# Gathering V rows 12 places behind U rows, with more places for the diagonal weights and earlier query products, in a one-core hybrid attention and PEER layer

## The chip, the cores and the metric

The kernel runs on one core of a Trainium2 chip. The metric is the device time of one execution in microseconds (us), and the number compared is the median over runs. Engines are named as in the profile: PE is TensorE (PEld its weight loads), DVE is VectorE, ACT is ScalarE, POOL is GpSimd, SP is SyncE.

## The reference

One decoder layer over 256 tokens of width 1024, in float32. Attention in two head groups, an output projection, then a product-key expert layer (PEER), which takes most of the time. For each of two chunks of 128 tokens:

```python
q = (xc @ w_query).reshape(PEER_CHUNK, PEER_HEADS, 2, PEER_D_HALF)
sc = jnp.einsum('chpd,hpnd->chpn', q, sub_keys)
s1, i1 = lax.top_k(sc[:, :, 0], 16)
s2, i2 = lax.top_k(sc[:, :, 1], 16)
...
best, pos = lax.top_k(cand, 16)           # of the 256 sums s1 + s2
experts = jnp.take_along_axis(cand_idx, pos, axis=-1)
g = jax.nn.softmax(best, axis=-1)
h = jax.nn.gelu(jnp.einsum('cd,chkd->chk', xc, u[experts]))
return jnp.einsum('chk,chkd->cd', h * g, v[experts])
```

Every token picks 16 experts for each of 8 heads, and each expert is one row of 1024 numbers in `u` and one in `v`. That is 256 gathered tiles of each (2 chunks, 8 heads, 16 choices), a tile being 128 tokens by 1024 numbers, 512 KB.

## The kernel before, in words

No scheduler orders the work: each engine's instructions are written out by hand and the engines meet at semaphores.

**Projection and attention** take the first 160 us or so. Near their end the work on experts begins, so that both overlap on every engine.

**A unit** is one head of one chunk: 16 units, each of 16 rows (gathered tiles), 256 rows in all. Rows are handled in groups of four. For row n the steps are these, each on its own engine and in the order of n:

1. POOL issues the gather of U row n (`gather_u`) into a ring of 10 places (`U_RING`). It waits until the dot product of row n-10 has been taken (`u_used`).
2. DVE takes the dot product of the row with the tokens (`dots`, L1190), after the row has landed, and counts `u_used` up.
3. ACT takes the GELU of a group of four (`gelu(g)`, L814), and DVE multiplies by the gates (`weights(g)`, L1203). DVE's order is `dots` of group g, `weights` of group g-1, then a part of `route`, which finds the experts of a later unit. So no dot product of group g+1 is taken before the GELU of group g-1.
4. ACT writes a 128x128 diagonal with the weight of row n (`diagonal(n)`, L821). ACT's order is `gelu(g)`, then the four diagonals of group g-1. There are 8 places for diagonals (`DIAG_RING`), so diagonal n waits until PE has finished row n-8 (`v_used`).
5. POOL issues the gather of V row n (`gather_v`). Its place is free when PE has finished the row that had it before: 11 rows earlier up to row 103, 13 rows earlier to row 159, and 16 from row 160 (`LATE`) on.
6. PE multiplies the diagonal with the V row into the output sums (`row_product`, L1569), two matmuls of 512 columns that the profile counts as two each, and counts `v_used` up. Five rows near the end (`ADDED_ROWS`) are added by DVE instead.

**POOL's order** is four gathers of U, then four of V, and so on. `LAG` says how far V is behind: the group of V after U rows g..g+3 is that of rows g-8..g-5.

**Queries.** A unit's experts need two query products (`query(e)`, L1487, 8 matmuls counted as 16), each evacuated by ACT (`query_evac`, L773), then a product with the keys (`key_scores`, L1470) and its evacuation (`scores_evac`, L767). Events e = 0 to 15 are the first chunk's, 2 for each head; 16 to 31 the second's. They stand between the row products. In the first chunk, heads 3 to 7 have theirs after rows 10 to 15 of units 0 to 4 on PE, and ACT evacuates two diagonals later. Head 2's (e = 4, 5) stand after rows 4 to 9. Those of the second chunk stand after rows 80 to 143, one event every four rows: query after row 4k, evacuation after diagonal 4k+1, key product after row 4k+2, its evacuation after diagonal 4k+3.

So PE waits for ACT's diagonals, ACT waits for PE's finished rows and queries, DVE waits for ACT's GELU, and POOL waits for both PE (V places) and DVE (U places).

## Time and profile before

| | |
|---|---|
| median of 3 runs | 907.79 us |
| lowest and highest | 902.74 and 909.92 us |
| the profiled execution's own time | 900.53 us |
| its span, first to last instruction | 898.7 us |
| PE, DVE, ACT, POOL busy, share of the span | 78%, 57%, 27%, 56% |
| bytes moved, mean rate | 297.88 MB, 331 GB/s |
| mean granted TensorE clock | 0.891 of 2.4 GHz |

The profile shows one execution. A busy share is over the whole span, and attention and gathers have different limits, so the stages are read one by one. POOL is counted as busy while it makes the descriptors of a gather. Idle time is put before the instruction that follows it, with what ended it; "remote" is the profile's word where it finds no instruction close enough to the release.

### The profile page before, as it was taken

The numbers are of one execution on the slowest core, as the hardware profiler recorded it, in microseconds if no ns is written. First come the engines' busy times: TensorE is split into PE (matmuls) and PEld (weight loads), VectorE is DVE, ScalarE is ACT, GpSimd is POOL, SyncE is SP. The second block draws the span as 40 slices with busy tenths as digits, with TensorE's granted clock in tenths as the row PEclk, the third lists the DMA queues.
The fourth block names the chain that finished last, engine by engine and source line by source line (L and its number), as shares of the span: only waits on it lengthen the run. The fifth ranks groups of instructions, "written<-read, shape, count | busy, mean of one in ns | idle before, by whom it ended". The sixth has DMA issues, their size and how long they took to land.

```text
span 898.7 us, 7608 instructions
## 1 busy us (share of the span) xinstructions
PE 699.5 (78%) x2208; PEld 376.9 (42%) x2208; DVE 510.1 (57%) x1395; ACT 243.0 (27%) x599; POOL 500.2 (56%) x533
## 2 busy tenths in 40 slices
PE   7989956879978877866686687788577857847877
PEld 5778645444434443433343343443233323312332
DVE  5754468638837474734554563557556764746643
ACT  6676434133131313012012121133030212121210
POOL 4000055646666666665654665556757666756763
PEclk9999988979999897968889998999769778968988
DMA  8856177989999999998987998979989999999996
GB/s 331 269 178 233 49 280 275 355 275 343 406 407 409 409 397 358 370 359 296 371 307 255 371 347 320 358 263 373 411 293 411 350 361 370 380 352 385 369 349 262
DMA packets 90087, 297.88 MB, mean 331 GB/s; under 512 B 8761, under 2 KB 14018, under 8 KB 90050
## 3 DMA queue, kind: packets, MB, share of 16 engines
q0 software_dynamic: 73728, 268.47, 79.6%
q1 hardware_dynamic: 16306, 28.97, 9.2%
q8 instruction: 16, 0.26, 0.1%
q14 instruction: 21, 0.17, 0.1%
q10 hardware_dynamic: 16, 0.00, 0.0%
HBM read 296.36 MB, written 1.05 MB: 331 GB/s over the span
## 4 chain that ended last, share of the span: by engine, by line
PE 60%; issue 15%; another core or an unknown queue 14%; ACT 6%; DVE 3%; DMA 1%; SPq 0%; DVEq 0%; ACTq 0%
PE bank L1569 44%; PE bank L1487 5%; PE bank L1301 4%; PE xg L1434 2%; PE bank L1434 2%; ACT diag L821 1%; DMA w_raw<-in_w_in_dram 1%; PE bank L1470 1%; DVE u_row L1190 1%; PE bank L1322 1%; PE bank L1350 1%; ACT soft L656 1%; ACT w_hi L601 1%; ACT L814 1%
## 5 line engine op out<-in xcount | busy, mean ns | idle before, releaser
L1569 PE MATMUL bank<-v_row,diag 128*128 128x512 f32 x1002 | 495.0, 643 | 148.7 <-issue 94.9
L1569 PEld LDWEIGHTS bank<-v_row,diag 128*128 128x128 f32 x1002 | 197.9, 206 | 398.1 <-issue 327.7
L541 POOL DMA_INDIRECT v_row<-in_peer_v_dram,expert x256 | 241.7, 944 | 179.1 <-remote 66.4
L527 POOL DMA_INDIRECT u_row<-in_peer_u_dram,expert x254 | 241.5, 951 | 109.2 <-issue 70.2
L1190 DVE CUSTOM_DVE_ANT_0 u_row<-u_row,xg 128x1024 f32<-128x1024 f32 x254 | 295.3, 1214 | 11.8 <-DMA u_row<-in_peer_u_dram,expert 8.3
L821 ACT ACTIVATE diag<-ident,act_w 128x128 f32<-128x128 f32 x251 | 87.6, 392 | 206.5 <-remote 87.2
L1203 DVE TENSOR_TENSOR act_w<-h_gelu,gate 128x4 f32<-128x4 f32 x64 | 10.5, 164 | 205.9 <-ACT h_gelu L814 121.5
L773 ACT ACTIVATE qT<-bank 128x128 f32<-128x128 f32 x32 | 8.8, 276 | 225.6 <-remote 178.7
L1487 PE MATMUL bank<-featT,wq_rest 128*128 128x128 f32 x192 | 29.6, 291 | 19.4 <-issue 19.2
L1487 PEld LDWEIGHTS bank<-featT,wq_rest 128*128 128x128 f32 x192 | 27.1, 204 | 27.7 <-issue 27.7
L428 POOL TENSOR_TENSOR normed<-qk_raw,t_qk_rs 128x512 f32<-128x512 f32 x4 | 4.1, 1048 | 56.5 <-DVE t_qk_rs L1026 56.5
L767 ACT ACTIVATE scores<-bank,t_rstd 128x128 f32<-128x128 f32 x32 | 11.8, 368 | 86.2 <-PE bank L1470 63.8
L1128 DVE MAX8 key_val<-scores 128x8 f32<-128x128 f32 x62 | 15.2, 283 | 34.4 <-issue 14.5
L1301 PE MATMUL bank<-w_hi,xn_hi 128*128 128x512 f32 x80 | 32.8, 410 | 2.4 <-ACT qk_raw L636 2.4
L1301 PE MATMUL bank<-w_hi,xn_lo 128*128 128x512 f32 x80 | 32.0, 400 | 0.0
L1301 PE MATMUL bank<-w_lo,xn_hi 128*128 128x512 f32 x80 | 31.8, 398 | 0.0
L902 DVE TENSOR_TENSOR w_lo<-w_raw,w_hi 128x2048 fp32r<-128x2048 f32 x11 | 25.2, 2287 | 8.4 <-ACT w_hi L601 8.4
L1470 PEld LDWEIGHTS bank<-skT,qT 128*128 128x128 f32 x64 | 14.1, 226 | 27.4 <-issue 20.7
L1487 PEld LDWEIGHTS bank<-featT,wq 128*128 128x128 f32 x192 | 23.4, 194 | 4.5 <-issue 4.4
L527 POOL DMA_INDIRECT u_first<-in_peer_u_dram,expert x2 | 2.1, 1050 | 41.1 <-DVE expert L1091 39.7
L814 ACT ACTIVATE h_gelu<-h_dot 128x4 f32<-128x4 f32 x64 | 12.5, 197 | 43.6 <-DVE h_dot L1190 36.5
L1487 PE MATMUL bank<-featT,wq 128*128 128x128 f32 x192 | 23.6, 277 | 0.0
(198 smaller groups left out, 624.7 us busy)
## 6 DMA issues: line engine op xcount, KB each, us to landing
w_raw<-in_w_in_dram SPq DMA_DIRECT2D x11, 1024.0 KB, 9.4
w_raw<-in_w_out_dram SPq DMA_DIRECT2D x4, 1024.0 KB, 5.1
v_row<-in_peer_v_dram,expert POOLq DMA_INDIRECT x256
u_row<-in_peer_u_dram,expert POOLq DMA_INDIRECT x254
wq<-in_peer_w_query_dram SPq DMA_DIRECT2D x3, 1024.0 KB, 9.2
wq_rest<-in_peer_w_query_dram SPq DMA_DIRECT2D x1, 3072.0 KB
x_sb<-in_x_dram SPq DMA_DIRECT2D x2, 512.0 KB, 4.8
w_raw<-in_w_in_dram SPq DMA_DIRECT2D x2, 512.0 KB, 6.4
```

Source lines behind the costliest of these rows:

```text
L527: pool.indirect_dma_start(u_row(n)[:, :], None, peer_u[0], bass.IndirectOffsetOnAxis(ap=expert[:, u, s:s + 1], axis=0))\
L541: pool.indirect_dma_start(v_row(n)[:, :], None, peer_v[0], bass.IndirectOffsetOnAxis(ap=expert[:, u, s:s + 1], axis=0))\
L814: act.activation(h_gelu[:, u % 4, s:s + GROUP], h_dot[:, u % 4, s:s + GROUP], ACT.Gelu).then_inc(gelu_done, 1)
L821: act.activation(diag[:, m % DIAG_RING, :], ident[:, :], ACT.Copy, scale=act_w[:, u % 4, s:s + 1])\
L902: dve.tensor_tensor(w_lo[:, j % W_PARTS, :, :].rearrange("p k n -> p (k n)"), w_raw[:, j % W_LOADS, :], w_hi[:, j % W_PARTS, :, :].rearran ...
L1128: at[a] = mark(dve.max(key_val[:, r2, a, top], score[a]))
L1190: dve.tensor_tensor_reduce(out=row[:, :], in0=row[:, :], in1=xg_row, scale=1.0, scalar=0.0, op0=ALU.mult, op1=ALU.add, accum_out=h_dot[:, ...
L1301: ins = mm(ps[bank][:, :], a[:, 4 * kh + k, h * P:(h + 1) * P], b[:, j % W_PARTS, k, :], start=kh == 0 and k == 0 and n == 0, stop=kh == 1 ...
L1434: ins = mm(ps[x2_bank(h, c)][:, :], mixT[h][:, 4 * kh + k, :], w_raw[:, j % W_LOADS, k * COLS:(k + 1) * COLS], start=h == 0 and kh == 1 an ...
L1470: mm(ps[2 + e % 2][:, 0:P], qT[:, e % 2, :], skT[:, hp, :], start=True, stop=True).then_inc(scores_done, 1)
L1487: ins = mm(ps[2 + e % 2][:, 0:P], wq_block(i, k, c), featT[h][:, k, :], start=k == 0, stop=k == KD - 1)
L1569: ins = mm(ps[y_bank(h, c)][:, :], diag[:, m % DIAG_RING, :], v_row(n)[:, c * COLS:(c + 1) * COLS], start=False, stop=True, skip_group_che ...
```

## The change

The lag of V behind U grows from 8 rows to 12. The diagonals get 12 places for rows before 160: the 8 of before (`diag_sq`) and 4 in the space of `mixed`, a tile of attention that is read for the last time by its last transposes. From row 160 there are 16: the first 8, and 8 more (`diag_freed`) in the space of a V place that the late rows don't use. At the crossing, diagonals 160 to 163 take places last used by rows 156 to 159. The queries and key products of head 2 stand ahead of all V rows on PE, and their evacuations ahead of the first GELU on ACT, with a wait for the last transposes of `mixed`. The queries of heads 3 to 7, and the transposes of the second chunk's features, stand four rows earlier. The queries of the second chunk stay where they were.

```diff
-DIAG_RING = 8
+DIAG_FIRST = 8
+DIAG_EARLY = 12
 GROUP = 4
-LAG = 8
+LAG = 12
...
-    diag = Region(sq_at).put("diag", [P, DIAG_RING, P])
+    diag_sq = Region(sq_at, sq_at + 4 * K).put("diag_sq", [P, DIAG_FIRST, P])
+    diag_mixed = Region(mixed_at, mixed_at + 2 * K).put("diag_mixed", [P, DIAG_EARLY - DIAG_FIRST, P])
...
+    freed = LATE - len(ring) + TOPK - 12
+    diag_freed = Region(v_row_at[v_place[freed]]).put("diag_freed", [P, TOPK - DIAG_FIRST, P])
+    diag_all = [diag_sq[:, i, :] for i in range(DIAG_FIRST)]
+    diag_all += [diag_mixed[:, i, :] for i in range(DIAG_EARLY - DIAG_FIRST)]
+    diag_all += [diag_freed[:, i, :] for i in range(TOPK - DIAG_FIRST)]
+    diag_turn = [m % DIAG_EARLY for m in range(LATE)]
+    diag_turn += [m % TOPK if m % TOPK < DIAG_FIRST else m % TOPK + DIAG_EARLY - DIAG_FIRST for m in range(LATE, GATHERS)]
+
+    def diag_before(m):
+
+        first = freed if diag_turn[m] >= DIAG_EARLY else -1
+        return max((i for i in range(m) if diag_turn[i] == diag_turn[m]), default=first)
...
-                need(act, v_used, m - DIAG_RING + 1)
+                need(act, v_used, diag_before(m) + 1)
...
+            act.wait_ge(probsT_done, MIXES_LAST + 1)
             d_deviation(1)
+            query_evac(4)
+            query_evac(5)
+            scores_evac(4)
+            scores_evac(5)
             for g in range(GROUPS + 1):
...
-                        if n == 56:
+                        if n == 52:
                             feat_evac(1, 0)
...
                         if 0 <= u <= 4:
                             e = 2 * (u + 3)
-                            if at == 10:
+                            if at == 6:
                                 query_evac(e)
-                            if at == 12:
+                            if at == 8:
                                 query_evac(e + 1)
-                            if at == 13:
+                            if at == 9:
                                 scores_evac(e)
-                            if at == 15:
+                            if at == 11:
                                 scores_evac(e + 1)
...
+            head_queries(2)
...
-                if n == 52:
+                if n == 48:
                     pe.wait_ge(scores_ready, 12)
...
                 if u <= 4:
                     e = 2 * (u + 3)
-                    if at == 10:
+                    if at == 6:
                         query(e)
```

The same shift of four rows is made for the other three places of the last hunk, and what stood for e = 4 and 5 after rows 4 to 9 is taken out on both engines.

POOL, the first gathers of V. `u_row` and `v_row` are the places of the two rings. Before:

```order
L527 DMA u_row0_136<-in_peer_u_dram,expert_93 128x1024
L527 DMA u_row1_137<-in_peer_u_dram,expert_93 128x1024
L541 DMA v_row0_148<-in_peer_v_dram,expert_93 128x1024
L541 DMA v_row1_149<-in_peer_v_dram,expert_93 128x1024
L541 DMA v_row11_159<-in_peer_v_dram,expert_93 128x1024
L541 DMA v_row12_160<-in_peer_v_dram,expert_93 128x1024
L527 DMA u_row2_138<-in_peer_u_dram,expert_93 128x1024
```

POOL, the same place of the changed kernel:

```order
L543 DMA u_row0_137<-in_peer_u_dram,expert_93 128x1024
L543 DMA u_row1_138<-in_peer_u_dram,expert_93 128x1024
L543 DMA u_row2_139<-in_peer_u_dram,expert_93 128x1024
L543 DMA u_row3_140<-in_peer_u_dram,expert_93 128x1024
L543 DMA u_row4_141<-in_peer_u_dram,expert_93 128x1024
L543 DMA u_row5_142<-in_peer_u_dram,expert_93 128x1024
L557 DMA v_row0_149<-in_peer_v_dram,expert_93 128x1024
```

The gathers of U rows 12 to 15 now stand ahead of V row 0, and every later group of V stands four U rows further back.

PE, from the identity products that end the attention to the first V rows. Before:

```order
L1547 MATMUL bank1<-scaled_108,ident_49 128x512
L1569 MATMUL bank0<-v_row0_148,diag_126 128x512
L1569 MATMUL bank1<-v_row0_148,diag_126 128x512
L1569 MATMUL bank0<-v_row1_149,diag_126 128x512
L1569 MATMUL bank1<-v_row1_149,diag_126 128x512
```

PE, the same place of the changed kernel:

```order
L1559 MATMUL bank1<-scaled_108,ident_49 128x512
L1499 MATMUL bank2<-featT0_122,wq2_low_132 128x128 x4
L1499 MATMUL bank2<-featT0_122,wq2_high_133 128x128 x4
L1499 MATMUL bank3<-featT0_122,wq2_low_132 128x128 x4
L1499 MATMUL bank3<-featT0_122,wq2_high_133 128x128 x4
L1482 MATMUL bank2<-skT_107,qT_81 128x128
L1482 MATMUL bank3<-skT_107,qT_81 128x128
L1582 MATMUL bank0<-v_row0_149,diag_sq_126 128x512
```

Head 2's two queries (`wq2`) and its two key products (`skT`) moved from between rows 4 and 9 to ahead of row 0.

ACT, from the first GELU on; `qT` is an evacuated query, `gexp` the exponential of the gates. Before:

```order
L814 ACTIVATE h_gelu_98<-h_dot_97 128x4 x2
L821 ACTIVATE diag_126<-ident_49,act_w_99 128x128 x4
L814 ACTIVATE h_gelu_98<-h_dot_97 128x4
L821 ACTIVATE diag_126<-ident_49,act_w_99 128x128 x3
L773 ACTIVATE qT_81<-bank2 128x128
L821 ACTIVATE diag_126<-ident_49,act_w_99 128x128
```

ACT, the same place of the changed kernel:

```order
L691 ACTIVATE t_d_sd_73<-t_d_ms_72 128x4
L789 ACTIVATE qT_81<-bank2 128x128
L789 ACTIVATE qT_81<-bank3 128x128
L783 ACTIVATE scores0_124<-bank2,t_rstd2_78 128x128
L783 ACTIVATE scores0_124<-bank3,t_rstd2_78 128x128
L830 ACT_TABLE_LOAD
L830 ACTIVATE h_gelu_98<-h_dot_97 128x4 x2
L837 ACTIVATE diag_sq_126<-ident_49,act_w_99 128x128 x4
L830 ACTIVATE h_gelu_98<-h_dot_97 128x4
L837 ACTIVATE diag_sq_126<-ident_49,act_w_99 128x128 x4
```

Four evacuations now stand ahead of the first GELU, and the first eight diagonals have no evacuation between them.

## Rows read from the trace of the kernel before

**Rows 1.** Page, costliest groups: busy, mean ns | idle before, what ended it.

```profile
L1569 PE MATMUL bank<-v_row,diag 128*128 128x512 f32 x1002 | 495.0, 643 | 148.7 <-issue 94.9
...
L541 POOL DMA_INDIRECT v_row<-in_peer_v_dram,expert x256 | 241.7, 944 | 179.1 <-remote 66.4
...
L1190 DVE CUSTOM_DVE_ANT_0 u_row<-u_row,xg 128x1024 f32<-128x1024 f32 x254 | 295.3, 1214 | 11.8 <-DMA u_row<-in_peer_u_dram,expert 8.3
```

**Rows 2.** Windows: length, PE PEld DVE ACT POOL busy, clock, DMA share, GB/s.

```profile
112.00:210.00 98.00, 71.81 (x313) 47.11 (x312) 64.45 (x217) 30.30 (x81) 53.92 (x58) 0.84 0.83 298
210.00:325.00 115.00, 101.98 (x287) 49.99 (x286) 70.86 (x207) 30.23 (x79) 76.21 (x81) 0.96 1.02 400
325.00:400.00 75.00, 54.36 (x162) 28.86 (x161) 41.37 (x117) 12.87 (x39) 50.23 (x54) 0.82 0.97 365
400.00:620.00 220.00, 166.70 (x559) 88.20 (x558) 115.33 (x329) 48.26 (x140) 126.44 (x136) 0.91 0.89 327
620.00:890.00 270.00, 196.92 (x401) 81.48 (x400) 157.87 (x406) 51.21 (x137) 178.50 (x187) 0.85 0.96 367
```

**Rows 3.** Groups on POOL, from 112 to 210 us.

```profile
L527 POOL DMA_INDIRECT u_row<-in_peer_u_dram,expert x32 | 30.1, 941 | 17.5 <-issue 7.9 <-DVE h_dot L1190 6.5 <-DVE expert L1167 2.4
L541 POOL DMA_INDIRECT v_row<-in_peer_v_dram,expert x24 | 22.6, 940 | 24.7 <-PE bank L1313 8.6 <-remote 6.0 <-issue 5.5
```

**Rows 4.** Groups on POOL, from 325 to 400 us.

```profile
L527 POOL DMA_INDIRECT u_row<-in_peer_u_dram,expert x27 | 25.8, 956 | 8.2 <-issue 7.3 <-DVE h_dot L1190 0.9
L541 POOL DMA_INDIRECT v_row<-in_peer_v_dram,expert x27 | 25.4, 940 | 16.9 <-issue 7.0 <-remote 6.6 <-PE bank L1569 3.3
```

**Rows 5.** Groups on POOL, from 400 to 620 us.

```profile
L527 POOL DMA_INDIRECT u_row<-in_peer_u_dram,expert x68 | 63.9, 940 | 37.9 <-issue 19.9 <-DVE h_dot L1190 18.0
L541 POOL DMA_INDIRECT v_row<-in_peer_v_dram,expert x68 | 63.9, 940 | 56.0 <-PE bank L1569 22.3 <-remote 19.0 <-issue 14.6
```

**Rows 6.** Groups on POOL, from 620 to 890 us.

```profile
L541 POOL DMA_INDIRECT v_row<-in_peer_v_dram,expert x99 | 94.1, 950 | 55.6 <-issue 29.1 <-remote 24.8 <-PE bank L1569 1.5
L527 POOL DMA_INDIRECT u_row<-in_peer_u_dram,expert x88 | 84.6, 961 | 33.7 <-issue 25.6 <-DVE h_dot L1190 8.1
```

**Rows 7.** Waits, 620 to 890 us: who waited for whom, total, times, longest.

```profile
POOL v_row L541 <- remote: 24.8, 10, 4.1
```

**Rows 8.** Timeline, 157 to 189 us: start, length, engine, what, idle before.

```profile
157.32 0.30 ACT L814 ACTIVATE h_gelu<-h_dot 128x4 f32<-128x4 f32 x2
157.52 3.32 PE L1547 MATMUL bank<-scaled,ident 128*128 128x512 f32 x4
...
159.21 0.94 POOL L527 DMA_INDIRECT u_row<-in_peer_u_dram,expert  x1 [1.90 <-DVE h_dot L1190]
...
170.16 1.06 PE L1487 MATMUL bank<-featT,wq_high 128*128 128x128 f32 x8
...
184.54 0.28 ACT L773 ACTIVATE qT<-bank 128x128 f32<-128x128 f32 x1 [19.44 <-remote]
...
188.19 0.16 DVE L1203 TENSOR_TENSOR act_w<-h_gelu,gate 128x4 f32<-128x4 f32 x1 [14.90 <-ACT h_gelu L814]
```

**Rows 9.** Timeline around query 21, 469 to 478 us: PE, ACT, POOL.

```profile
469.75 1.06 PE L1487 MATMUL bank<-featT,wq_high 128*128 128x128 f32 x8
...
477.52 0.28 ACT L773 ACTIVATE qT<-bank 128x128 f32<-128x128 f32 x1 [10.85 <-remote]
...
477.81 0.94 POOL L541 DMA_INDIRECT v_row<-in_peer_v_dram,expert  x1 [2.71 <-remote]
```

**Rows 10.** Timeline, 791 to 802 us: ACT and POOL.

```profile
791.76 0.40 ACT L821 ACTIVATE diag<-ident,act_w 128x128 f32<-128x128 f32 x1 [10.09 <-issue]
...
796.98 0.94 POOL L527 DMA_INDIRECT u_row<-in_peer_u_dram,expert  x1 [0.30 <-issue]
...
801.62 0.40 ACT L821 ACTIVATE diag<-ident,act_w 128x128 f32<-128x128 f32 x1 [9.37 <-remote]
...
801.80 0.94 POOL L541 DMA_INDIRECT v_row<-in_peer_v_dram,expert  x1 [3.88 <-remote]
```

More of the change, by code:

```diff
@@ L75 @@
 MIX_AFTER = {0: 0, 4: 1, 6: 4}
+MIXES_LAST = max(MIXES_READY)
 D_VALUES = [1, 5]
@@ L819, in diagonal @@
                 m = multiplied(n)
-                need(act, v_used, m - DIAG_RING + 1)
-                act.activation(diag[:, m % DIAG_RING, :], ident[:, :], ACT.Copy, scale=act_w[:, u % 4, s:s + 1])\
+                need(act, v_used, diag_before(m) + 1)
+                act.activation(diag_all[diag_turn[m]], ident[:, :], ACT.Copy, scale=act_w[:, u % 4, s:s + 1])\
                    .then_inc(diag_ready, 1)
@@ L876, in _ @@
                                 scores_evac(e)
-                        if n == GATHERS // 2 + DIAG_RING:
+                        if n == GATHERS // 2 + DIAG_FIRST:
                             for c in range(2):
@@ L1568, in row_product @@
                 for c in range(2 if n < GATHERS - 1 else 1):
-                    ins = mm(ps[y_bank(h, c)][:, :], diag[:, m % DIAG_RING, :],
+                    ins = mm(ps[y_bank(h, c)][:, :], diag_all[diag_turn[m]],
                              v_row(n)[:, c * COLS:(c + 1) * COLS],
@@ L1593, in _ @@
                     x2_transposes(1, 1)
-                if n == 57:
+                if n == 53:
                     pe.wait_ge(featT_ready[0], 3)
-                if n == 4:
-                    query(4)
-                if n == 6:
-                    query(5)
-                if n == 7:
-                    key_scores(4)
-                if n == 9:
-                    key_scores(5)
                 if u <= 4:
                     e = 2 * (u + 3)
-                    if at == 10:
+                    if at == 6:
                         query(e)
-                    if at == 12:
+                    if at == 8:
                         query(e + 1)
-                    if at == 13:
+                    if at == 9:
                         key_scores(e)
-                    if at == 15:
+                    if at == 11:
                         key_scores(e + 1)
```

9 lines of the change are left out of this document (removed).

## The prediction

> **What bounds the kernel now.** I first read the costliest groups [rows 1] to find the long stage: 256 gathers of V, as many of U, 254 listed dot products, and 1002 listed matmuls (about 250 rows of four) that PE is busy with for 495 us, 1.98 us a row. None of that fills the span of 898.7 us. Next come the windows [rows 2], which tell where the transfers are full. From 210 to 325 us they run at 400 GB/s with a DMA share of 1.02: there the gathers themselves are the bound. Elsewhere it is 298, 365, 327 and 367 GB/s, so something keeps POOL from issuing.
>
> What that is worth can be counted. One gather takes POOL 0.94 us plus 0.30 us of idle time before it even where nothing is waited for [rows 1, 10], 1.24 us together. Idle time beyond 0.30 us a gather is true waiting. From 112 to 210 us (56 gathers) it is 42.2 - 16.8 = 25.4 us [rows 3]; from 325 to 400 us (54) 25.1 - 16.2 = 8.9 us [rows 4]; from 400 to 620 us (136) 93.9 - 40.8 = 53.1 us [rows 5]; from 620 to 890 us (187) 89.3 - 56.1 = 33.2 us [rows 6]. In the last stage nearly all of it stands before V gathers, and ten waits on "remote" hold 24.8 us, the longest 4.1 us [rows 7].
>
> What is POOL waiting for there? ACT makes one diagonal at 791.76 us and the next only at 801.62, after 9.37 us of waiting; then POOL, idle since 797.92, gets its V place at 801.80 [rows 10]. Diagonal and place both wait for rows that PE has finished. A query's matmuls end at 470.81 us, ACT takes the result at 477.52, and POOL's V place comes at 477.81 after 2.71 us of idling [rows 9]. So what PE has done is told to the others up to 7 us late while POOL issues without a break, and comes through some 3 us after POOL has stopped. The Trainium skill (TensorE: Matmul & The Clock Gate, "The cost: per-tile semaphore tail") gives tens of nanoseconds for a matmul's semaphore increment. By that, ACT would have gone on at about 470.9; this trace shows 6.7 us more, and the row decides. I take the lateness as given, whatever makes it: the places are then a stock on which POOL lives until the news arrives.
>
> **The change part by part, against the profiled execution's 900.5 us.** The median of the runs is 907.79, or 1.008 times that.
>
> *Queries of head 2 ahead of all V rows.* Removed: ACT's wait for query 4, 19.44 us until 184.54, in whose shadow DVE waited 14.90 us for a GELU [rows 8]. Added: ACT's first GELU, at 157.32 before, now comes behind four evacuations, and these behind PE's identity products, which end at 160.84 [rows 8]. Two queries follow: half of one is 1.06 us [rows 8], so 4.2 us by the rows; consecutive halves overlap a little, and I take 3.7. Then key product, evacuations and a table load, which I estimate at 2.5 us, so the GELU runs at about 167, 10 us late. Behind it stand the weights of group 0 and the dot product of row 8, on which the gather of U row 18 depends; that row was issued at 159.21 [rows 8] and now comes at about 168.8. In the new order POOL has by 157 us issued what needs no GELU, U rows 0 to 17 and V rows 0 to 3, 22 gathers, and idles 12 us. From 168.8 it can go on without a wait, since the experts of unit 2 are found early and ACT has no evacuation among the first eight diagonals: to 208.7 us that is 39.9 / 1.245 + 1 = 33, or 55 in all. Before, 57 were issued by then, among them the 56 of [rows 3]. Two gathers less are 2.5 us. Bounds: if the wait for query 4 simply returns elsewhere, the 12 us stay lost; if the twelve places spare a later wait of this stage, 5 us are won. I take +2.
>
> *210 to 325 us.* The transfers are full [rows 2], so neither lag nor places matter: 0. A gather only comes earlier or later in the stream.
>
> *325 to 400 us, and the start of the next stage.* A V place waits for PE's row 11 back, and in the new order POOL has issued four more U gathers when it gets to that V gather. A stretch between two long waits holds about 16 gathers (54 issued in 3 to 4 stretches), then 20. If each wait is still some 3 us long, 4/20 of 8.9 us go, 1.8. The same holds for the first 40 us of the next stage, until row 104 has 13 places: a fifth of 53.1 us, of which another fifth goes, 2.1. Together -4; between 0 and -13.
>
> *400 to 620 us, queries of the second chunk.* These stay where they are, and ACT is never more than two rows ahead of PE there. When ACT waits for the query after row 4k, the GELU of group k+1 is done, so DVE can take dot products up to row 4k+15 and POOL can issue U up to row 4k+25. With the lag of 8, POOL stops at V row 4k+13, having issued U to 4k+23: 8k+37 gathers. With 12 it stops at U row 4k+26, having issued V to 4k+11: 8k+38. The wait changes its name from V to U and nothing is won: 0; between +5 (POOL four V gathers behind where DVE sets the pace) and -10.
>
> *620 to 890 us, 16 diagonals.* Here no evacuation ties ACT to PE. With 8 places ACT stops 8 rows ahead of the last row it has been told of; PE then runs dry too, and the news that ends the wait brings few rows. With 16, PE works on, so that each release frees more places, and the lag adds four U gathers to each stretch. Ten remote waits [rows 7], several of them in pairs, are about eight stretches of 187 / 8 = 23 gathers. I take 12 more a stretch, between 4 (the lag alone) and 20: 33.2 x 12/35 = 11.4 us. Bounds: 4/27 of it, 5 us, and all of it, 33 us. At the crossing, diagonals 160 to 163 wait for rows 156 to 159: one wait of the usual 3 us, within these bounds.
>
> *The end.* Twelve V gathers instead of eight follow the last U gather, but the number of all gathers is the same, and the last V row waits for no dot product: 0. *Other edits:* the wait for the last transposes of `mixed` is met before it is reached, since ACT has evacuated later ones. Moving queries of heads 3 to 7 up by four rows keeps the scores as early as before against the U rows, though V is later: 0, and without it DVE would wait for scores by four rows, 10 us a unit.
>
> Sum: +2 - 4 + 0 - 11.4 = -13.4, so 887.1 us for the execution and 894.3 for the median, taken as 894.
>
> **The rivals.** *The wait only changes its name everywhere.* U has 10 places still, and DVE's dot products wait for GELUs that stand behind diagonals. If these set the pace in the last stage too, what remains is the start, +2, and some saving of the middle: 900 or so, 908 as a median. For it speaks that in the stage at 400 to 620 us U gathers wait 18.0 us for dot products [rows 5]; against it that from 620 on it is 8.1 us [rows 6].
>
> *Slower: the start is not regained.* POOL's 12 idle us stand just ahead of the stage in which transfers are full. If the news of PE's rows is late again among rows 6 to 11, where head 3's queries now stand, the stretch from 168.8 to 208.7 us has two waits of 3 to 4 us that I left out, and the stage at 400 us gives the +5. Then 900.5 + 2.5 + 7 + 5 - 2 = 913, or 920 as a median. It decides from one such wait on, if the last stage gives only its 5 us.
>
> *The waits of the last stage go altogether,* if the news is late by a fixed time and the longer stock outlasts it: 900.5 + 2 - 4 - 33 = 865.5, as a median 872. Against it: the waits are all near 3 us, up to 4.1 at most [rows 7], though the stretches differ, which looks like an end that POOL's own pause brings.
>
> *No room in the transfers.* If memory gave about 350 GB/s at most, all stages from 325 us on would be full and only the start would count, 903, or 910 as a median. The Trainium skill (DMA: Bandwidth & Descriptors, "Where 436 GB/s comes from") says that about 358 GB/s per core binds such loads. The windows show 400 over 115 us [rows 2], so I give this little.
>
> **How the numbers follow.** Runs of this kernel differ by 0.8% between lowest and highest, so 1% is about what a measurement can tell. Forecast (all with 1 to 2.5% gained) 0.41; waits gone altogether 0.12; only the name changes 0.25; no room 0.03; slower 0.19. Faster by over 1% is 0.41 + 0.12 = 0.53; within 1%, 0.25 + 0.03 = 0.28; slower 0.19. The range takes in most of the case of 872 and ends between the unchanged time and 920: 873 to 914.
>
> **What would show each step.** Right: POOL idle from about 157 to 168 us, then no wait over 1 us until 200; ACT without a wait of over 10 us before 200; from 400 to 620 us the idle time before V gathers falls and that before U gathers rises by as much, the sum within 10 us; from 620 on, waiting beyond 0.30 us a gather is near 22 us, with stretches over 30 gathers, and ACT's diagonals wait far less. Wrong: POOL's waits before 210 us add up to over 30 us; or the last stage still has ten remote waits; or the rate there stays at 367 GB/s with POOL never waiting.

## The result: slower, 948.83 us against 907.79

The changed kernel takes 948.83 us (median of 5 runs, 936.89 to 949.47). Against the kernel before on the same chip that is 1.044, 95% interval 1.038 to 1.050. The forecast was 894 us, in a range of 873 to 914. The profiled execution is that of the median and has a span of 947.0 us, 48.3 us more than before, and a mean granted clock of 0.873 after 0.891. (The medians are only 41.0 us apart, since the profiled execution of the kernel before was 7 us faster than its median.)

The costliest groups of the changed kernel, which answer to [rows 1] (L543 gathers U, L557 gathers V, L1202 takes the dot products, L830 the GELU, L1215 makes the weights, L789 evacuates a query):

```profile
L543 POOL DMA_INDIRECT u_row<-in_peer_u_dram,expert x254 | 240.4, 946 | 218.2 <-DVE h_dot L1202 145.2
...
L557 POOL DMA_INDIRECT v_row<-in_peer_v_dram,expert x256 | 242.4, 947 | 117.7 <-issue 70.7
...
L1215 DVE TENSOR_TENSOR act_w<-h_gelu,gate 128x4 f32<-128x4 f32 x64 | 10.5, 164 | 227.3 <-ACT h_gelu L830 206.4
...
L789 ACT ACTIVATE qT<-bank 128x128 f32<-128x128 f32 x32 | 8.9, 277 | 295.7 <-remote 234.9
```

Before, the longer idle time stood ahead of the V gathers (179.1 us, [rows 1]). Now it stands ahead of the U gathers, and two thirds of it end with a dot product of DVE. DVE waited 206.4 us for GELUs, and ACT, which makes them, 234.9 us for "remote" at its query evacuations. As the timeline further down shows, those are the links of one chain. The windows answer to [rows 2]:

```profile
112.00:210.00 98.00, 66.27 (x290) 43.82 (x289) 59.27 (x201) 29.00 (x75) 48.17 (x51) 0.79 0.76 279
210.00:325.00 115.00, 98.10 (x273) 47.31 (x273) 70.47 (x207) 25.67 (x72) 72.52 (x78) 0.94 0.97 373
325.00:400.00 75.00, 55.61 (x165) 27.99 (x163) 38.96 (x106) 14.71 (x39) 47.68 (x51) 0.91 0.94 353
400.00:640.00 240.00, 170.39 (x556) 91.10 (x556) 113.05 (x314) 44.25 (x131) 122.74 (x131) 0.86 0.77 288
640.00:935.00 295.00, 211.96 (x419) 87.06 (x419) 166.63 (x434) 57.16 (x156) 192.63 (x202) 0.82 0.95 363
```

Windows of two kernels don't hold the same work. So I counted POOL's 512 gathers in their order in both traces and read when the n-th was issued; the difference of two columns says where the time went:

| n-th gather | before | after | later by | added in this stretch |
|---|---|---|---|---|
| 60 | 212.4 | 220.7 | 8.3 | 8.3 |
| 100 | 269.3 | 277.7 | 8.4 | 0.1 |
| 200 | 417.3 | 437.6 | 20.3 | 11.9 |
| 300 | 574.4 | 611.1 | 36.7 | 16.4 |
| 340 | 637.8 | 684.1 | 46.3 | 9.6 |
| 400 | 724.4 | 769.7 | 45.3 | -1.0 |
| 512 | 886.6 | 931.9 | 45.3 | 0.0 |

8 us are lost by the 60th gather and 38 from the 100th to the 340th, in which the queries lie. The last stage begins at about the 340th gather. I hoped to win 11 us in it, and from there to the last gather it takes 248.8 us before and 247.8 after. From the last gather to the end of the span it is 12.1 us before and 15.1 after. The waits of the changed kernel from 400 to 640 us show the chain (who waited for whom, total, times, longest):

```profile
DVE act_w L1215 <- ACT h_gelu L830: 131.4, 12, 18.6
ACT qT L789 <- remote: 94.6, 7, 18.8
POOL u_row L543 <- DVE h_dot L1202: 84.3, 22, 16.1
...
POOL v_row L557 <- PE bank L1582: 1.5, 5, 0.3
```

Here are POOL's groups from 112 to 210 us, then from 400 to 640, then from 640 to 935; they answer to [rows 3], [rows 5] and [rows 6]:

```profile
L543 POOL DMA_INDIRECT u_row<-in_peer_u_dram,expert x30 | 28.2, 941 | 31.8 <-DVE h_dot L1202 24.4 <-issue 6.8 <-PE bank L1313 0.6
L557 POOL DMA_INDIRECT v_row<-in_peer_v_dram,expert x20 | 19.0, 951 | 10.6 <-issue 5.8 <-remote 4.8
...
L543 POOL DMA_INDIRECT u_row<-in_peer_u_dram,expert x66 | 62.1, 940 | 97.8 <-DVE h_dot L1202 84.3 <-issue 13.4
L557 POOL DMA_INDIRECT v_row<-in_peer_v_dram,expert x65 | 61.3, 942 | 19.8 <-issue 18.3 <-PE bank L1582 1.5
...
L557 POOL DMA_INDIRECT v_row<-in_peer_v_dram,expert x108 | 102.7, 951 | 55.4 <-issue 29.6 <-remote 21.5 <-PE bank L1582 4.4
L543 POOL DMA_INDIRECT u_row<-in_peer_u_dram,expert x94 | 89.9, 957 | 44.8 <-issue 24.7 <-DVE h_dot L1202 17.6 <-remote 2.6
```

In the query stage the waits for PE's rows, 22.3 + 19.0 us before [rows 5], are down to 1.5; those for dot products are up from 18.0 to 84.3. The wait did change its name, as forecast, but it became longer in doing so: beyond 0.30 us a gather it is 117.6 - 131 x 0.30 = 78.3 us for 131 gathers, after 53.1 for 136.

One stop shows why. This is the timeline around query 21 (engine, what, idle time before):

```profile
486.97 0.97 PEld L1499 LDWEIGHTS bank<-featT,wq_high 128*128 128x128 f32 x8
487.08 1.06 PE L1499 MATMUL bank<-featT,wq_high 128*128 128x128 f32 x8
...
496.22 0.94 POOL L543 DMA_INDIRECT u_row<-in_peer_u_dram,expert  x1 [0.30 <-issue]
500.16 0.28 ACT L789 ACTIVATE qT<-bank 128x128 f32<-128x128 f32 x1 [16.17 <-remote]
...
505.03 0.37 ACT L783 ACTIVATE scores<-bank,t_rstd 128x128 f32<-128x128 f32 x1 [4.01 <-PE bank L1482]
505.41 1.28 ACT L824 ACT_TABLE_LOAD   x1
...
506.94 1.28 ACT L830 ACT_TABLE_LOAD   x1
508.23 0.21 ACT L830 ACTIVATE h_gelu<-h_dot 128x4 f32<-128x4 f32 x1
...
508.47 0.16 DVE L1215 TENSOR_TENSOR act_w<-h_gelu,gate 128x4 f32<-128x4 f32 x1 [18.20 <-ACT h_gelu L830]
...
511.81 1.21 DVE L1202 CUSTOM_DVE_ANT_0 u_row<-u_row,xg 128x1024 f32<-128x1024 f32 x1
...
513.30 0.94 POOL L543 DMA_INDIRECT u_row<-in_peer_u_dram,expert  x1 [16.14 <-DVE h_dot L1202]
```

PE's query ends at 488.14. POOL goes on issuing until 497.16, and 3.0 us after it has stopped ACT gets the news, 12.0 us after the query's end. With that news the stop is not over: POOL stands at a U gather, and a U place comes free last of all, after the evacuation, the key product, the scores (505.03), two table loads of 1.28 us, the GELU (508.23), the weights and DVE's next top-k work (until 511.81) and the dot product. That is 13.1 us behind the news. Before, around the same query, POOL stood at a V gather and went on 0.29 us after ACT had the news, 477.81 after 477.52 [rows 9]. This is not the one case: nine query evacuations of the kernel before are followed by a V gather that ends a wait 0.29 or 0.30 us later, while in the changed kernel four late ones (at 427.31, 500.16, 585.66 and 617.70 us) are followed by a U gather 9.0 to 13.1 us later. By the order of the program the next V gathers stand behind the U gather in POOL's one queue, though the next two, rows 112 and 113, need no row of PE after row 100, which was done ahead of the query.

### The profile page after: what moved, and what is told of

Same layout as the page of the kernel before. It is cut to its first block, busy times and chain, and to the rows that moved or that the text cites. A ratio compares the mean times of both kernels' runs of the same rounds, so it can differ in the third digit from the quotient of the medians.

```text
span 947.0 us, 7608 instructions
## 1 busy us (share of the span) xinstructions
PE 713.8 (75%) x2208; PEld 380.5 (40%) x2208; DVE 511.8 (54%) x1395; ACT 241.1 (25%) x599; POOL 499.9 (53%) x533
## 3 DMA queue, kind: packets, MB, share of 16 engines
HBM read 296.36 MB, written 1.05 MB: 314 GB/s over the span
## 4 chain that ended last, share of the span: by engine, by line
PE 51%; issue 17%; another core or an unknown queue 15%; DVE 9%; ACT 4%; DMA 2%; POOL 1%; SPq 0%; DVEq 0%; ACTq 0%
PE bank L1582 35%; DVE u_row L1202 5%; PE bank L1313 4%; PE bank L1499 4%; PE xg L1446 1%; PE bank L1382 1%; DMA v_row<-in_peer_v_dram,expert 1%; PE bank L1362 1%; POOL u_row L543 1%; PE bank L1334 1%; PE bank L1482 1%; ACT diag_sq L837 1%; DMA x_sb<-in_x_dram 1%; ACT L830 1%
## 5 line engine op out<-in xcount | busy, mean ns | idle before, releaser
L1582 PE MATMUL bank<-v_row,diag_sq 128*128 128x512 f32 x624 | 314.1, 651 | 110.6 <-ACT diag_sq L837 58.8
L543 POOL DMA_INDIRECT u_row<-in_peer_u_dram,expert x254 | 240.4, 946 | 218.2 <-DVE h_dot L1202 145.2
L1202 DVE CUSTOM_DVE_ANT_0 u_row<-u_row,xg 128x1024 f32<-128x1024 f32 x254 | 296.7, 1215 | 37.7 <-DMA u_row<-in_peer_u_dram,expert 34.6
L557 POOL DMA_INDIRECT v_row<-in_peer_v_dram,expert x256 | 242.4, 947 | 117.7 <-issue 70.7
L1582 PEld LDWEIGHTS bank<-v_row,diag_sq 128*128 128x128 f32 x624 | 125.2, 208 | 266.1 <-issue 196.4
L1582 PE MATMUL bank<-v_row,diag_freed 128*128 128x512 f32 x170 | 97.0, 698 | 48.9 <-issue 48.9
L1215 DVE TENSOR_TENSOR act_w<-h_gelu,gate 128x4 f32<-128x4 f32 x64 | 10.5, 164 | 227.3 <-ACT h_gelu L830 206.4
L1582 PE MATMUL bank<-v_row,diag_mixed 128*128 128x512 f32 x208 | 104.9, 639 | 29.6 <-issue 18.8
L789 ACT ACTIVATE qT<-bank 128x128 f32<-128x128 f32 x32 | 8.9, 277 | 295.7 <-remote 234.9
L837 ACT ACTIVATE diag_sq<-ident,act_w 128x128 f32<-128x128 f32 x156 | 53.5, 391 | 119.5 <-remote 78.9
L1582 PEld LDWEIGHTS bank<-v_row,diag_freed 128*128 128x128 f32 x170 | 36.8, 217 | 106.8 <-issue 106.1
L1582 PEld LDWEIGHTS bank<-v_row,diag_mixed 128*128 128x128 f32 x208 | 40.2, 204 | 76.2 <-issue 63.6
L830 ACT ACTIVATE h_gelu<-h_dot 128x4 f32<-128x4 f32 x64 | 12.7, 200 | 96.8 <-issue 58.7
L1499 PEld LDWEIGHTS bank<-featT,wq_rest 128*128 128x128 f32 x192 | 24.4, 197 | 11.0 <-issue 11.0
L1499 PE MATMUL bank<-featT,wq_rest 128*128 128x128 f32 x192 | 24.6, 279 | 3.7 <-issue 3.6
```

Of the source, the lines that this page charges most:

```text
L543: pool.indirect_dma_start(u_row(n)[:, :], None, peer_u[0], bass.IndirectOffsetOnAxis(ap=expert[:, u, s:s + 1], axis=0))\
L557: pool.indirect_dma_start(v_row(n)[:, :], None, peer_v[0], bass.IndirectOffsetOnAxis(ap=expert[:, u, s:s + 1], axis=0))\
L830: act.activation(h_gelu[:, u % 4, s:s + GROUP], h_dot[:, u % 4, s:s + GROUP], ACT.Gelu).then_inc(gelu_done, 1)
L837: act.activation(diag_all[diag_turn[m]], ident[:, :], ACT.Copy, scale=act_w[:, u % 4, s:s + 1])\
L1202: dve.tensor_tensor_reduce(out=row[:, :], in0=row[:, :], in1=xg_row, scale=1.0, scalar=0.0, op0=ALU.mult, op1=ALU.add, accum_out=h_dot[:, ...
L1215: dve.tensor_tensor(act_w[:, u % 4, s:s + GROUP], h_gelu[:, u % 4, s:s + GROUP], gate[:, u % 2, s:s + GROUP], ALU.mult).then_inc(act_ready, 1)
```

## Experiments

Theory A is what the timeline suggests: with V 12 rows behind, POOL meets a U gather at the stops of the query stage, and U waits for the longest chain. The rivals: the start (head 2's queries ahead) carries the cost (B), or the places of the diagonals do (C).

**The parts alone, on a chip where the kernel before takes 801.75 us.** c1 is the changed kernel with `LAG = 8`. c2, c3 and c4 are the kernel before with one part of the change each: the distance, head 2's queries ahead (what stood for them after rows 4 to 9 is taken out), and the places of the diagonals.

```diff
-LAG = 12
+LAG = 8
```

> The changed kernel with the lag of V put back from 12 to 8, all else as changed. Theory A (with the longer lag POOL stops at a U gather, which is set free last in the chain of late rows, diagonals, GELU, dot product, while V places that are free stand behind it): the loss of 41 us goes, 900 to 915 us, and U gathers wait under 25 us for dot products between 400 us and V row 160. Theory B (the loss is made at the start, by head 2's queries ahead of the first GELU, and by the queries moved up): stays at 930 to 950 us. Theory C (with more places ACT and DVE run ahead and get in PE's way): 930 to 950 us.

```diff
-LAG = 8
+LAG = 12
```

> The kernel before with the lag of V alone set to 12; 8 places for diagonals and all queries where they were. Theory A: 940 to 965 us, at least as slow as the changed kernel, since scores also come four rows late against U. Theory B: 900 to 915 us. Theory C: 900 to 915 us.

```diff
             d_deviation(1)
+            query_evac(4)
+            query_evac(5)
+            scores_evac(4)
+            scores_evac(5)
...
             head_queries(1)
...
+            head_queries(2)
```

> The kernel before with head 2's queries, key products and evacuations alone moved ahead of all V rows and of the first GELU. Theory A: 903 to 915 us, the first GELU some 10 us later, most of it regained by 210 us. Theory B: 930 us or more. Theory C: as before, within 5 us.

```diff
-                need(act, v_used, m - DIAG_RING + 1)
-                act.activation(diag[:, m % DIAG_RING, :], ident[:, :], ACT.Copy, scale=act_w[:, u % 4, s:s + 1])\
+                need(act, v_used, diag_before(m) + 1)
+                act.activation(diag_all[diag_turn[m]], ident[:, :], ACT.Copy, scale=act_w[:, u % 4, s:s + 1])\
```

> The kernel before with the places for diagonals alone changed, 12 to row 159 and 16 from there. Theory A: 893 to 908 us, less waiting of ACT from 620 us on and a little won there. Theory B: as before, within 5 us. Theory C: 930 us or more.

Measured against the kernel before: c1 1.005 (1.003 to 1.007), c2 1.007 (1.005 to 1.010), c3 1.005 (1.003 to 1.008), c4 1.000 (0.999 to 1.001). The expectations were set for 908 us and missed in all their times. None of the theories is told from the others here: on this chip there is little to lose.

**Both kernels on another chip of that kind** (the kernel before 801.48 us), unchanged:

> The changed kernel itself, run beside the kernel before on the chip of this call. If the 4.4% belong to the change wherever it runs: ratio 1.04. If they come from PE's finished work being told late, which the four runs so far don't show (a query is evacuated 0.04 us after its last matmul in each of 30 cases of the run with lag 8, and the kernel before takes 801.75 us there): about the sum of the lag alone and the start alone, ratio 1.01, 808 to 813 us, as long as this chip tells PE's work at once; and 1.04 if it tells it late.

> The kernel before, unchanged, for its trace on this chip. If PE's work is told at once: 800 to 803 us, transfers at about 409 GB/s from 210 us to the end, and no query evacuated more than 1 us after its last matmul. If it is told late: 900 to 912 us and a trace like the first one.

The changed kernel takes 1.011 (1.009 to 1.013) of the time before, the kernel before again 1.000. The timeline of the kernel before on this chip, at a query:

```profile
409.99 1.06 PE L1487 MATMUL bank<-featT,wq_high 128*128 128x128 f32 x8
...
411.08 0.28 ACT L773 ACTIVATE qT<-bank 128x128 f32<-128x128 f32 x1 [5.53 <-PE bank L1487]
```

and its window from 400 to 620 us:

```profile
400.00:620.00 220.00, 179.33 (x546) 88.10 (x545) 147.89 (x401) 55.30 (x156) 160.95 (x171) 0.97 1.03 409
```

ACT takes the query 0.04 us after its matmuls end, in the middle of POOL's issuing, and so it is at every query from the fifth on. Transfers run at 409 GB/s (327 in [rows 2]) and bound the kernel. So the lateness that I took as given is seen on some chips and not on others, and where it is seen the kernel takes some 100 us more. That the lateness makes all of these is not shown: the granted clock differs as well, 0.940 here and 0.891 in the first trace. Even here the mechanism is seen once, started by another delay; the changed kernel's timeline:

```profile
368.67 2.56 PE L1582 MATMUL bank<-v_row,diag_mixed 128*128 128x512 f32 x4 [4.11 <-DMA v_row<-in_peer_v_dram,expert]
...
374.10 0.28 ACT L789 ACTIVATE qT<-bank 128x128 f32<-128x128 f32 x1 [15.85 <-PE bank L1499]
...
378.25 0.16 DVE L1215 TENSOR_TENSOR act_w<-h_gelu,gate 128x4 f32<-128x4 f32 x1 [9.75 <-ACT h_gelu L830]
...
381.91 0.94 POOL L543 DMA_INDIRECT u_row<-in_peer_u_dram,expert  x1 [6.99 <-DVE h_dot L1202]
```

PE waited 4.11 us for a V row to land, the query behind it came later by that, and POOL stopped at a U gather for 6.99 us.

**Making the news late on purpose.** If the lateness is what the cost hangs on, it should appear where it is put in. A detour: SP waits for PE's signal and sends a DMA of 64 B; POOL's V gathers and ACT's diagonals (where they wait for rows from 80 on) and the 16 query evacuations of the second chunk wait for its landing instead. e1 is the kernel before with this detour, e2 the changed kernel, e3 the changed kernel with `LAG = 8`.

```diff
-                need(pool, v_used, v_before(n) + 1)
+                need_row(pool, v_before(n) + 1)
...
-                act.wait_ge(query_done, e + 1)
+                if e >= HP:
+                    act.wait_ge(told_query[e % 4], 16 * ((e - HP) // 4 + 1))
+                else:
+                    act.wait_ge(query_done, e + 1)
...
+                sp.wait_ge(seen, value)
...
+                sp.dma_start(relay[at:at + 1, 16 * slot:16 * slot + 16], x[0, 0:1, 0:16]).then_inc(told_on, 16)
```

> The kernel before, in which from the 80th row on the news of PE's finished work goes by a detour: SP waits for v_used (and for query_done of the second chunk) and passes it on by a small DMA of 64 B whose landing POOL's V gathers, ACT's diagonals and ACT's query evacuations wait for. Nothing of the work changes; what PE has finished is known to POOL and ACT some us later. Theory A (the cost is lateness times the length of the chain that a stopped U gather hangs on): V places and diagonals come free late but the V gathers stop in small pieces, as on the first chip; 1.00 to 1.02 of the kernel before. The rival (late news costs both kernels the same): the same 1.00 to 1.02 here, so this run is the base for the next two.

> The changed kernel with the same detour. Theory A: the ratio to the kernel before grows clearly past the 1.011 of the changed kernel without a detour, and more than that of the kernel before with the detour grows past 1: 1.025 to 1.045, with POOL's waits for DVE's dot products at U gathers each after a run of 16 gathers between 380 and 620 us. The rival (late news costs both the same, the 4.4% of the first chip came from something else): 1.011 plus what the detour costs the kernel before, within 0.005.

> The changed kernel with LAG = 8 and the same detour: V eight rows behind U again, the diagonals and the start as changed. Theory A: 8 rows behind undo most of what the detour adds to the changed kernel; the ratio comes within 0.008 of the kernel before with the detour. If the diagonals or head 2's queries carry the cost under late news, it stays near the changed kernel with the detour.

Measured, the kernel before at 800.25 us: e1 1.032 (1.030 to 1.035), e2 1.052 (1.048 to 1.056), e3 1.041 (1.038 to 1.044). With the detour a query of the second chunk is taken 1.2 to 4.7 us after its last matmul. POOL's groups from 400 to 620 us, of e1, then e2, then e3:

```profile
L565 POOL DMA_INDIRECT u_row<-in_peer_u_dram,expert x78 | 73.1, 937 | 26.1 <-issue 16.5 <-DVE h_dot L1231 9.7
L579 POOL DMA_INDIRECT v_row<-in_peer_v_dram,expert x78 | 73.1, 937 | 49.0 <-DMA relay<-in_x_dram 23.8 <-issue 19.8 <-DVE h_dot L1231 5.4
...
L581 POOL DMA_INDIRECT u_row<-in_peer_u_dram,expert x74 | 69.8, 944 | 62.4 <-DVE h_dot L1243 49.0 <-issue 13.4
L595 POOL DMA_INDIRECT v_row<-in_peer_v_dram,expert x74 | 69.3, 937 | 22.6 <-issue 22.6
...
L581 POOL DMA_INDIRECT u_row<-in_peer_u_dram,expert x77 | 72.4, 940 | 25.9 <-issue 18.9 <-DVE h_dot L1243 7.0
L595 POOL DMA_INDIRECT v_row<-in_peer_v_dram,expert x76 | 71.5, 941 | 51.3 <-DMA relay<-in_x_dram 25.1 <-issue 23.7 <-DVE h_dot L1243 2.5
```

This is the picture of the first chip, made smaller on a chip that doesn't have it: at 8 rows behind POOL waits for V places, at 12 only for dot products, and longer (49.0 us against 23.8 + 5.4 + 9.7 and 25.1 + 2.5 + 7.0). The changed kernel's distance to the kernel before grows from 1.1% to 1.9% (1.052 / 1.032); that of e3 is 0.8%, at the edge of the 0.008 expected. So of the 1.9%, 1.1 hang on the distance. The direction is Theory A's, but the sizes were missed: 1.052 lies above its 1.025 to 1.045, and e1 had gone past its 1.02. A detour of 1.2 to 4.7 us does not make 4.4%.

**The queries' news alone, and later news.** f1 (the kernel before) and f2 (the changed kernel) detour the query evacuations alone; SP still sends its DMAs for the rows, so what these cost is in the result. f3 and f4 (again before and changed) have the whole detour, but a row is told with the last of its four only, and a query behind the next row. These four ran on a chip of the first pair's kind: the kernel before took 899.98 us.

```diff
-                need_row(pool, v_before(n) + 1)
+                need(pool, v_used, v_before(n) + 1)
...
-                need_row(act, m - DIAG_RING + 1)
+                need(act, v_used, m - DIAG_RING + 1)
```

> The kernel before with the detour for the 16 query evacuations of the second chunk alone: V gathers and diagonals wait for PE's own signal again; SP's small DMAs for the rows are still sent, but nobody waits for them. If the query's step (query, qT, key scores, scores, then the GELU behind it on ACT) carries what late news costs, this stays near the 1.032 of the full detour (1.02 or more); if late V places carry it, it is within 1.005 of 1.

> The changed kernel with the detour for the second chunk's query evacuations alone. Theory A, in the form that a stopped U gather hangs on the query's step and V has reserve: 1.035 to 1.052, most of what the full detour costs the changed kernel, and more above the kernel before with the same detour than the 1.1% without any. If the rows' news are what the difference hangs on, it comes within 0.005 of 1.011.

```diff
-                i = value - TOLD_FROM - 1
+                i = min((value - TOLD_FROM - 1) | 3, multiplied(GATHERS) - TOLD_FROM - 1)
```

> The kernel before with the detour, and the news made later: a V row's place and diagonal are told with the last row of its four only, a query with the row behind it (one row is about 2.5 us). Theory A: the kernel before loses more than by the plain detour, 1.04 to 1.07, the V gathers stopping first.

> The changed kernel with the same later news. Theory A (cost is lateness times the chain of a stopped U gather): its distance to the kernel before with the same news grows beyond the 1.9% of the plain detour, to 2.5 to 4%. The rival (a fixed difference, the places of the changed kernel being enough to hide the rest): it stays at 1 to 2% or shrinks, since diagonals have 12 and 16 places.

Measured: f1 1.027 (1.018 to 1.036), f2 1.073 (1.065 to 1.081), f3 1.077 (1.065 to 1.089), f4 1.091 (1.082 to 1.101). The detour of the queries alone, with SP's DMAs, costs the kernel before 2.7%. The distance of f2 to f1 is 4.5% (1.073 / 1.027), about the 4.4% of the first pair over again: on a chip with late news it does not grow by the detour, and f2 lies above the 1.035 to 1.052 expected. And f4 stands only 1.3% above f3, where Theory A expected 2.5 to 4. The intervals of the two overlap, and f3's four runs spread from 961.61 to 978.51 us, so the 1.3% is rough; but nothing here bears out the form "cost is lateness times chain". With news in fours POOL stops at V gathers of f3 for 87.0 us of the 220 from 400 on. I take it that the advantage of stopping at V is used up there.

f2 also shows who is told late, since here SP waits for PE as well. The timeline of SP's queue, from 488 to 512 us, then from 504 to 508, then ACT and POOL:

```profile
488.52 18.05 SPq L521 DMA_DIRECT2D relay<-in_x_dram  x5
...
506.01 0.57 SPq L521 DMA_DIRECT2D relay<-in_x_dram  x2
...
502.12 0.94 POOL L573 DMA_INDIRECT u_row<-in_peer_u_dram,expert  x1 [0.30 <-issue]
509.27 0.28 ACT L822 ACTIVATE qT<-bank 128x128 f32<-128x128 f32 x1 [19.48 <-DMA relay<-in_x_dram]
...
521.95 0.94 POOL L573 DMA_INDIRECT u_row<-in_peer_u_dram,expert  x1 [18.89 <-DVE h_dot L1235]
```

PE's query had ended at 493.94; SP passed nothing on between 494 and 506, and its next two messages left from 506.01 on, 2.95 us after POOL's last gather before them ended at 503.06. (The view merges the five messages of its first line into one of 18.05 us.) SP's other wait, for the landing of an earlier message, was over by 492.47. So SP, too, hears of PE's work only when POOL has paused: the lateness is not one of ACT's or POOL's receiving alone.

**The parts alone again, on a chip of the first kind** (the kernel before 897.21 us), with the edits of c2 and c1:

> The kernel before with LAG = 12 alone, as c2, again, for the case that this chip tells PE's work late (the kernel before near 900 us): then Theory A (the distance carries the cost, since a stopped U gather waits for the longest chain) expects 1.03 to 1.05; if the start or the diagonals carry it, 1.01. Where the kernel before is near 800 us: 1.007 as before.

> The changed kernel with LAG = 8, as c1, again, for the same case. Theory A on a chip with late news: 1.00 to 1.015, most of the 4.4% gone. If the start (head 2's queries ahead) or the diagonals carry the 4.4%: 1.03 or more. Where the kernel before is near 800 us: 1.005 as before.

Measured: **g1, the distance alone, 1.077** (1.068 to 1.085), above the 1.03 to 1.05 expected; **g2, everything but the distance, 1.004** (1.000 to 1.009), within its 1.00 to 1.015. POOL's groups from 400 to 620 us, of g1, then of g2:

```profile
L541 POOL DMA_INDIRECT v_row<-in_peer_v_dram,expert x61 | 57.2, 937 | 23.1 <-issue 17.7 <-remote 4.8 <-PE bank L1569 0.6
L527 POOL DMA_INDIRECT u_row<-in_peer_u_dram,expert x60 | 56.2, 937 | 84.9 <-DVE h_dot L1190 71.3 <-issue 13.6
...
L557 POOL DMA_INDIRECT v_row<-in_peer_v_dram,expert x68 | 63.7, 936 | 57.8 <-PE bank L1582 27.4 <-remote 15.5 <-issue 14.9
L543 POOL DMA_INDIRECT u_row<-in_peer_u_dram,expert x67 | 63.0, 940 | 38.2 <-issue 19.2 <-DVE h_dot L1202 19.0
```

One number in the source, 12 for 8, moves the stops from V to U, and 121 gathers go out in 220 us where 135 did. From the 200th to the 340th gather g1 takes 255.3 us and g2 226.3; from there to the last they take 249.9 and 248.9. That decides for the distance, against B and C: the start and the places together cost 0.4% here (0.0 to 0.9), a tenth of the 4.4. With the distance of 12 they give back some of what the distance costs, 7.7% down to 4.4 (measured on two chips), 8.8 us of it by the 100th gather (286.5 in g1, 277.7 in the changed kernel). In that stretch the wait that I had removed, query 4's, stands in g1's timeline with a U gather behind it:

```profile
190.22 0.28 ACT L773 ACTIVATE qT<-bank 128x128 f32<-128x128 f32 x1 [28.17 <-remote]
...
204.65 0.94 POOL L527 DMA_INDIRECT u_row<-in_peer_u_dram,expert  x1 [18.96 <-DVE h_dot L1190]
```

How much of what they give back is the places and how much the earlier queries was not tried.

**The other way.** The kernel before with a distance of 4 (e4, on the chip of e1, and h1), and the changed kernel with 4 (h2). Both chips were of the faster kind (the kernel before at 800.25 and at 800.71 us).

```diff
-LAG = 8
+LAG = 4
```

> The kernel before with LAG = 4: V gathers four rows behind U, the way opposite to the change, nothing else. Theory A, on a chip that tells PE's work at once: a stop costs only where the transfers run dry, and a V row that has landed early waits for its diagonal longer, so V places stop more often; 0.995 to 1.01. If a shorter distance goes on helping, below 0.995; a rival (each row of distance costs 0.2% at the end of the kernel, because four V gathers and their products stand behind the last U row): 0.993, 4 rows of 2 x 1.25 us less after the last U gather.

> The kernel before with LAG = 4, as e4. Theory A: the V gathers stand nearer behind their U gathers, so a stop falls on V even more often; where the news is late (the kernel before near 900 us) it expects 0.985 to 1.005, since the V gathers, with fewer landed rows in reserve, stop sooner but release sooner. The rival (both stops cost the same; the distance of 12 is only past the reach of the places): 0.995 to 1.02, worse than LAG = 8, since V places stay taken while their diagonals are missing. Where the kernel before is near 800 us: 1.002 as before.

> The changed kernel with LAG = 4: the diagonals' places and head 2's queries as changed, the distance 4. Whether more diagonals help a short distance: with 8 rows behind they were worth nothing (1.004 with the start on the late chip), and with 12 rows behind the changed kernel stood at 1.044 against 1.077 of the distance alone. Theory A: within 0.01 of h1, plus or minus the start's 0.005. A version that beats both kernels would show here or in h1 as under 0.99.

Measured: e4 1.002 (1.001 to 1.004), h1 1.003 (1.002 to 1.004), h2 1.004 (1.002 to 1.006). So on the faster kind 8 is the best of the three distances, by a little (12: 1.007), and no version ran faster than the kernel before by more than the noise (c4, 1.000, comes nearest). What 4 does where the news is late stays open.

## Why the prediction was wrong

**The failed step is the term of the query stage**, "the wait changes its name from V to U and nothing is won: 0; between +5 and -10". The count behind it (8k+37 gathers against 8k+38) was right: in the changed kernel each of the seven stops of over 7 us between 400 and 660 us comes when 8k+38 gathers are out (198, 222, 238, 254, 286, 302 and 318), and in the kernel before the long stops at V come within two gathers of 8k+37. But I counted how many gathers go out before a stop and took it that every stop ends alike. Its end is what differs: a V place comes with PE's news, 0.3 us after ACT has it; a U place 9 to 13 us later. From the 200th to the 340th gather 26.0 us are lost, five times my bound. g1 and g2 show that the distance is the cause; that it acts by this chain is read from the timelines and from e2, where the waits move to U as soon as the news is late.

The size of the lateness was misread as well. I wrote "up to 7 us late" from one query; in the same trace the query that ends at 372.48 us is evacuated at 389.12, 16.6 us later. None of my terms had a lateness of that size.

**325 to 400 us, -4:** the same step, taken with the wrong sign. I gave each wait "some 3 us" by the V waits of [rows 4], and saw the stretches grow; from the 100th to the 200th gather (269 to 417 us before) 11.9 us are lost.

**The start, +2:** 8.3. The GELU ran at 160.32 rather than 167, and POOL went on at 162.21 rather than 168.8, better than I had worked out. But the slower rival's condition came true. The changed kernel's timeline:

```profile
201.26 0.28 ACT L789 ACTIVATE qT<-bank 128x128 f32<-128x128 f32 x1 [29.08 <-remote]
...
201.55 0.94 POOL L557 DMA_INDIRECT v_row<-in_peer_v_dram,expert  x1 [4.83 <-remote]
...
212.03 0.94 POOL L543 DMA_INDIRECT u_row<-in_peer_u_dram,expert  x1 [8.29 <-DVE expert L1179]
```

Head 3's query, now among rows 6 and 8, waits for late news as head 2's did (29.08 us after 19.44 in [rows 8]), and the weights, top-k work and experts of unit 2 behind it come at 211.76, where I had them "found early". On a chip without lateness c3 shows 0.5% for this part alone.

**The last stage, -11.4:** -1.0 from the 340th gather on. The stretches did not grow as I took it. With stops of over 1 us counted, those within eight gathers as one, POOL stops eight times in these 172 gathers before and seven times after, so a mean stretch goes from 22 to 25 gathers, where I had 23 and 35. The waits of the changed kernel from 640 to 935 us:

```profile
ACT diag_sq L837 <- remote: 78.9, 11, 27.3
...
POOL v_row L557 <- remote: 21.5, 6, 5.6
...
POOL u_row L543 <- DVE h_dot L1202: 17.6, 12, 7.5
```

The remote waits at V fell from ten to six, but they last up to 5.6 us rather than 4.1 [rows 7]: 21.5 us after 24.8. Waiting beyond 0.30 us a gather is 55.4 + 44.8 - 202 x 0.30 = 39.6 us in this window, where I said 22. But the window holds a stop of 7.5 us at 657 us that still belongs to the queries. From the 340th gather on the same sum is 32.5 us before and 31.7 after. (Of the 33.2 us before, 7.3 stood before U gathers, in one wait of 7.2, so "nearly all of it stands before V gathers" was too much said.) ACT's remote waits for diagonals are fewer and longer (11, the longest 27.3 us, after 19 of up to 10.1), and yet the 16 places and the lag together won POOL no more than the 1.0 us. I had written that the lateness ends with POOL's pause, and still priced each wait at its old length. That a longer stock of places only makes the news later is how I read this; it was not tried by itself. c4 (1.000, the places alone) and g2 (1.004, with the start) show it worth nothing at 8 rows behind, on either kind of chip.

**The end, 0:** +3.0 us behind the last gather. What of it the four more V rows make was not tried.

**The rivals.** "Only the name changes" was right on where the waits of the query stage go and wrong on what they cost. The slower rival had the start right (its condition came true, and its 2.5 + 7 us stand against the measured 8.3), but it again capped the query stage at +5, so 920 fell short by 29 us. That the waits vanish, or that 350 GB/s bound the kernel, is refuted: 373 GB/s from 210 to 325 us here, 409 on the chips of the faster kind. The Trainium skill's figure of about 358 GB/s per core (DMA: Bandwidth & Descriptors, "Where 436 GB/s comes from") lies below both. The Trainium skill's tens of nanoseconds for a semaphore increment (TensorE: Matmul & The Clock Gate, "The cost: per-tile semaphore tail") agree with the 0.04 us of those chips, not with the 12.0 us here.

## What to carry to other kernels

Where one in-order queue issues for several rings, ask at each stop which ring it stands at, and follow the chain from the event that ends the stop to that ring's release; counting how far the queue gets before it stops is half of the sum. Here a larger distance moved the stop to the ring that is released last, and what was free behind it waited too. And run a change on more than one chip when the profile shows a lateness that nothing in the program explains: here one kernel takes 801 or 900 us, and the same change costs 1.1% or 4.4%.

## What the runs showed of the hardware

- The kernel before took 800 to 802 us on four chips, 897 and 900 on two others, and 908 in the first comparison. On the slower kind, PE's finished work is known to ACT, POOL and SP up to 16.6 us late (a query of the kernel before; 22.9 in the changed kernel) while POOL issues gathers without a break. In most of the late cases the news comes 1 to 5 us after the end of POOL's last gather before a stop; some, 3.8 to 10.1 us late, came while POOL was still issuing or within 0.4 us of it (391.65 and 427.31 us in the changed kernel). On the faster kind it is known after 0.04 us, with POOL issuing just the same. Whether signal or product is late the traces can't tell, and what sets the kinds apart stays open.
- Transfers reach 409 GB/s over hundreds of us on the faster kind, with 171 gathers of 512 KB in 220 us, one each 1.29 us. On the slower kind they reached 400 over 115 us [rows 2].
- A signal that is passed on by a DMA of 64 B arrived 1.2 to 4.7 us after the work it tells of, among saturated transfers (e1 to e3).
